# Output projections of a two-layer block: pairs of row tiles in seven quadrant products, with the gate row in the weights

## The reference, cut to what matters

```python
mix = jnp.concatenate([att, mlstm_out(h_sum, mo, mlstm_norm_w)], -1)
x = x + g1 * (mix @ w_out)                        # 2048 x 1024 by 1024 x 1024, g1 one row of 1024
hx2 = modulate(rmsnorm(x, norm2_w), sh2, sc2)
aff = jax.nn.softmax((h @ w_router).astype(f32), -1)   # in the expert layer, h = hx2
```

## Time and profile before

| | us |
|---|---|
| median of 3 runs | 4071.45 |
| lowest and highest run | 4067.83, 4078.97 |
| span of the profiled execution | 4066.4 |
| PE busy | 3776.7 (93%) |
| DVE busy | 1951.9 (48%) |
| ACT busy | 1561.1 (38%) |
| POOL busy | 547.7 (13%) |

### The profile page before, as it was taken

How to read it: one execution, slowest core, us unless ns; L and a number is a source line. 1 busy time by engine, 2 the same in 40 slices (tenths; PEclk the granted TensorE clock), 3 DMA queues, 4 the chain that set the end, 5 groups by cost and what they waited for, 6 DMA issues and landing times. The chain is left out here.

```text
span 4066.4 us, 63104 instructions
## 1 busy us (share of the span) xinstructions
PE 3776.7 (93%) x21839; PEld 2444.1 (60%) x21840; DVE 1951.9 (48%) x4191; ACT 1561.1 (38%) x3432; POOL 547.7 (13%) x746
## 2 busy tenths in 40 slices
PE   6999999799898978999999799997999999599998
PEld 4667766555584434777777677774666555344444
DVE  1334334556585553111111278776333444578886
ACT  1122211355564431111111266764333222267775
POOL 0000000100170010111111001101000000322222
PEclk8999999899999998999999899998999999699999
DMA  6222122222525477656656212115231133498974
GB/s 240 76 78 82 70 76 79 87 72 85 142 95 199 158 265 292 201 168 211 200 168 217 70 47 66 56 52 148 67 107 39 35 131 117 181 318 277 331 240 101
DMA packets 227153, 573.85 MB, mean 141 GB/s; under 512 B 28154, under 2 KB 100986, under 8 KB 211118
## 3 DMA queue, kind: packets, MB, share of 16 engines
q1 hardware_dynamic: 177742, 395.92, 27.7%
q0 software_dynamic: 49248, 175.79, 14.6%
HBM read 433.59 MB, written 137.93 MB: 141 GB/s over the span
## 5 line engine op out<-in xcount | busy, mean ns | idle before, releaser
L880 PE MATMUL inp_psU<-inp_w,inp_hT 128*128 128x512 f32 (+3 forms) x1376 | 420.8, 464 | 0.0
L880 PEld LDWEIGHTS inp_psU<-inp_w,inp_hT 128*128 128x128 f32 x1376 | 256.0, 190 | 152.7 <-issue 122.4
L4286 DVE COPY moe_bu<-moe_wu 128x1024 f32 x480 | 299.2, 697 | 39.2 <-DMA moe_wd<-in_w_down 22.5
L4173 PE MATMUL moe_psU<-moe_bu,shared_weights 128*32 128x256 f32 x3840 | 294.8, 382 | 0.9 <-issue 0.9
L4173 PE MATMUL moe_psU<-moe_wu,shared_weights 128*32 x1280 | 293.2, 382 | 1.8 <-DVE moe_bu L4286 1.7
L876 PE MATMUL inp_psU<-inp_hT,inp_w 128*128 128x256 f32 x1088 | 245.7, 386 | 10.2 <-DVE inp_tm L682 4.5
L2807 ACT ACTIVATE moe_sg<-moe_psG 128x256 f32<-128x256 f32 x64 | 24.6, 384 | 567.0 <-PE moe_psG L2766 567.0
L2824 DVE TENSOR_TENSOR moe_hT<-moe_sg,moe_psG 128x256 f32<-128x256 f32 x64 | 26.9, 421 | 437.7 <-ACT moe_sg L2807 437.7
L876 PEld LDWEIGHTS inp_psU<-inp_hT,inp_w 128*128 128x128 f32 x1088 | 209.0, 194 | 42.7 <-ACT inp_fm L773 3.9
L3502 PE MATMUL inp_psU<-shared_weights,inp_w 128*128 128x256 f32 x1024 | 231.9, 382 | 2.7 <-DMA inp_wg<-in_lru_wx 2.7
L2766 PE MATMUL moe_psG<-moe_xT,moe_u_w 128*128 128x256 f32 x1024 | 231.5, 379 | 0.0
(11 more groups left out here) (702 smaller groups left out, 7149.7 us busy)
## 6 DMA issues: line engine op xcount, KB each, us to landing
moe_wu<-in_w_up SPq DMA_DIRECT2D x32, 2048.0 KB
moe_d_w<-in_w_down SPq DMA_DIRECT2D x16, 2048.0 KB, 10.4
moe_wd<-in_w_down SPq DMA_DIRECT2D x32, 1024.0 KB
moe_u_w<-in_w_up SPq DMA_DIRECT2D x15, 2048.0 KB, 13.5
mod_w<-in_w_ada SPq DMA_DIRECT2D x24, 1024.0 KB, 13.2
inp_mod_w<-in_w_mod SPq DMA_DIRECT2D x16, 1024.0 KB, 4.9
xn<-out_xn POOLq DMA_DIRECT2D x32, 512.0 KB, 3.8
shared_weights<-in_w_gate SPq DMA_DIRECT2D x8, 2048.0 KB, 8.6
```

The lines of the kernel that those rows point to most:

```text
L880: mm = pe.matmul(psU[:, u % NB, 0:n], hT[:, par, k, j * P:(j + 1) * P], w[:, k, lo:lo + n], start=(k == 0), stop=(k == KD - 1))
L4173: mm = pe.matmul(psU[c, f, 0:2 * P], xT[:, p, k, c], w, start=(k == 0), stop=(k == KD - 1), tile_position=(0, g * LOT))
L4286: ins = dve.tensor_copy(bu[:, g - 1, f, c, :].rearrange("p k n -> p (k n)").unsqueeze(1), wu[:, bass.ds(slots[g - 1], 1), f, c, :].rearran ...
```

## The change

Tiles 0 and 1 are computed as before. From tile 2 on the tiles go in pairs (a, b), and the pair's product of 2 x 2 quadrants (two tiles by the two halves of `mixT`; the two halves of the weights' rows by two halves of columns) is made in seven products of quadrants in place of eight (Winograd's form of Strassen's scheme). Write Ad, An for tile a's direct and normed half, Bd, Bn for tile b's, and D0, D1, N0, N1 for the weights' quadrants. The row sums are left0 = Bd + Bn, left1 = left0 - Ad, left2 = An - left1, left3 = Ad - Bd (in place of Bd). The column sums, made once, are t1 = D1 - D0, t2 = N1 - t1, t4 = N0 - t2 and N1 - D1 (in place of D1). TensorE's products and VectorE's joins:

| product | of | joined into |
|---|---|---|
| P1 | Ad, D0 | part 0 (a copy) |
| P2 | An, N0 | x of a, columns 0 |
| P6 | left1, t2 | part 1 = P1 + P6 |
| P7 | left3, N1 - D1 | part 2 = part 1 + P7 |
| P5 | left0, t1 | part 3 = part 1 + P5, and x of b, columns 1 = part 2 + P5 |
| P3 | left2, N1 | x of a, columns 1 = part 3 + P3 |
| P4 | Bn, t4 | x of b, columns 0 = part 2 + P4 |

(In the scheme P4 carries a minus, which t4's sign takes in.) GpSimd makes the four row sums of each pair (`make_left`) and adds the residual x (`add_x`), which VectorE did. The gate row is no longer multiplied on each tile: at the stage's start VectorE multiplies it into the direct weights and GpSimd into the normed ones. `norm` is split into `square_mix` and `scale_mix`, `rest` into the joins and `finish`. All loops over tiles are written out. The modulation ring has 10 blocks in place of 12 and lends three of them for t1, t2 and t4 in out1, so that seven are loaded at its end and three after the last product. In layer 1 the gate row is loaded in the stage before, into the second row of the `x` buffer, so tile 1's x is loaded after the weights are multiplied.

```diff
-    RING = 12
+    RING, LENT = 10, 3
...
-        self.mix, self.mixT = tile("mix", [P, 2, 512]), tile("mixT", [P, 2, KD, P])
+        self.mix, self.mixT = tile("mix", [P, 2, 512]), tile("mixT", [P, 4, KD, P])
...
@@ VectorE @@
+            def room(t):
+
+                if t >= 2:
+                    dve.wait_ge(x_stored[t % 2], 32 * (t // 2))
+
+            def finish(t):
+                j = t % 2
+                if t < 2:
+                    dve.wait_ge(taken, 2 * t + 2)
+                else:
+                    dve.wait_ge(x_added, t - 1)
                 dve.tensor_tensor_reduce(out=sq[:, :], in0=xo[:, j, :], in1=xo[:, j, :], scale=1.0 / D,
...
+            dve.wait_ge(gr_landed, 16)
+            dve.wait_ge(direct_weights_landed, 32)
+            for h in range(2):
+                dve.tensor_tensor(w_direct[:, :, cols[h]], w_direct[:, :, cols[h]], gr[:, cols[h]].unsqueeze(1).to_broadcast([P, KH, BANK]),
+                                  ALU.mult).then_inc(direct_scaled, 1)
...
+            for q in range(1, PAIRS):
...
+                dve.wait_ge(made, made_by(q, P1))
+                if q > 1:
+                    dve.wait_ge(summed, 4 * q - 4)
+                dve.tensor_copy(part[:, 0, :], bank(q, P1)).then_inc(parted, 1)
+                room(a)
+                join(q, P2, xo[:, 0, cols[0]], part[:, 0, :], summed, n + 1)
+                if more:
+                    square_mix(c)
...
+                join(q, P6, part[:, 1, :], part[:, 0, :], parted, n + 1)
+                if more:
+                    scale_mix(c)
+                join(q, P7, part[:, 2, :], part[:, 1, :], parted, n + 2)
+                if more:
+                    square_mix(d)
...
+                join(q, P5, part[:, 3, :], part[:, 1, :], parted, n + 2)
+                room(b)
+                join(q, P5, xo[:, 1, cols[1]], part[:, 2, :], summed, n + 3)
+                if more:
+                    scale_mix(d)
+                join(q, P3, xo[:, 0, cols[1]], part[:, 3, :], summed, n + 4)
+                finish(a)
+                join(q, P4, xo[:, 1, cols[0]], part[:, 2, :], summed, n + 4)
+                finish(b)
@@ ScalarE @@
+            for q in range(1, PAIRS):
...
+                keep_turned(a - 2)
+                if more:
+                    gate(c)
+                    gate(d)
+                    root_mix(c)
...
+                keep_across(a - 2)
+                keep_turned(b - 2)
+                keep_logits(a - 2)
+                if more:
+                    root_mix(d)
+                    keep_mix(c)
...
+                keep_across(b - 2)
+                if more:
+                    keep_mix(d)
+                root_x(a)
+                keep_logits(b - 2)
+                root_x(b)
@@ TensorE @@
+            for q in range(1, PAIRS):
...
+                multiply(q, P1, direct_of(a), w_direct[:, :, cols[0]])
+                turn_xn(a - 2)
...
+                multiply(q, P2, normed_of(a), w_normed[:, :, cols[0]])
...
+                multiply(q, P6, left[:, 1, :, :], t2)
+                route_across(a - 2)
...
+                multiply(q, P7, direct_of(b), w_direct[:, :, cols[1]])
+                turn_xn(b - 2)
+                route(a - 2)
+                multiply(q, P5, left[:, 0, :, :], t1)
+                if more:
+                    turn(c)
+                multiply(q, P3, left[:, 2, :, :], w_normed[:, :, cols[1]])
+                route_across(b - 2)
+                if more:
+                    turn(d)
+                multiply(q, P4, normed_of(b), t4)
+                route(b - 2)
@@ GpSimd @@
+            def add_x(t):
+                q, j = t // 2, t % 2
+                pool.wait_ge(summed, 4 * q if j else 4 * q - 1)
+                pool.wait_ge(x_landed[j], nth(t))
+                pool.tensor_tensor(xo[:, j, :], xo[:, j, :], x[:, j, :], ALU.add).then_inc(x_added, 1)
...
+                pool.tensor_tensor(left[:, 0, :, :], direct_of(b), normed_of(b), ALU.add).then_inc(left_made, 1)
...
+            store(0)
+            for q in range(1, PAIRS):
+                store(2 * q - 1)
+                add_x(2 * q)
+                if q + 1 < PAIRS:
+                    make_left(q + 1)
+                add_x(2 * q + 1)
+                if q == PAIRS - 1:
+                    pool.drain()
+                store(2 * q)
+            store(NT - 1)
```

More of the change, by code:

```diff
@@ L1998, in out_projection @@
         fold = s.sb("fold", [P, n_logits])
+        left = s.sb("left", [P, 3, KH, P])
+        right = ring.lent() if ring else s.sb("right", [P, 3, KH * BANK])
+        t1, t2, t4 = (right[:, n, :].rearrange("p (k n) -> p k n", k=KH) for n in range(3))
         early_choice = RowChoice(nc, s, "early", 0, EARLY_ROWS, logits_out, picks) if picks else None
@@ L2020, in out_projection @@
[L2020 to L2035, removed]
+        direct, normed = rows.direct, 4 - rows.direct
@@ L2092, in norm, with scale_mix @@
                                   ).then_inc(msq, 1)
+            def scale_mix(t):
+                j = t % 2
+                ch = Chain(dve, dch, t, NF, NF - 3 if layer == 1 else NF - 2)
+                hv = mix[:, j, :]
+                hg = hv.rearrange("p (g d) -> p g d", g=NG)
                 dve.wait_ge(rooted, t + 1)
@@ new lines, in _ @@
+            square_mix(2)
+            scale_mix(2)
+            dve.wait_ge(normed_scaled, 2)
+            dve.wait_ge(right_dve, 1)
+            dve.tensor_tensor(t2, w_normed[:, :, cols[1]], t1, ALU.subtract).then_inc(right_dve, 1)
+            square_mix(3)
+            scale_mix(3)
+            for t in range(2):
+                first_rest(t)
+            for q in range(1, PAIRS):
+                a, b, c, d = (2 * q + n for n in range(4))
+                more = q + 1 < PAIRS
+                n = 4 * (q - 1)
+                dve.wait_ge(made, made_by(q, P1))
[6 more added lines that the diff above has]
+                    square_mix(c)
+                elif picks:
@@ L2203, in product @@
[L2203 to L2208 removed]
+                    pe.wait_ge(direct_scaled, h + 1)
+                    for k in range(KH):
+                        pe.matmul(psO[:, t, h, :], direct_of(t)[:, k, :], w_direct[:, k, cols[h]], start=(k == 0), stop=False)
@@ L2215, in product, with multiply @@
                 mm.then_inc(made, 1)
-            def turn(t, j):
+            def multiply(q, i, lhs, rhs):
+                n = 4 * (q - 1)
+                if q == 1 and i <= P7:
+                    pe.wait_ge(taken, i + 1)
+                elif i == P1:
+                    pe.wait_ge(parted, n - 1)
+                elif i in (P2, P6, P7):
+                    pe.wait_ge(summed, n - 3 + i)
+                elif i == P3:
+                    pe.wait_ge(summed, n + 1)
+                else:
+                    pe.wait_ge(parted, n + 1 if i == P5 else n + 2)
+                for k in range(KH):
+                    mm = pe.matmul(bank(q, i), lhs[:, k, :], rhs[:, k, :], start=(k == 0), stop=(k == KH - 1))
+                mm.then_inc(made, 1)
```

392 lines of the change are left out of this document (236 added, 156 removed).

## The result

The changed kernel takes 4087.74 us (median; 4086.49 to 4090.64), the kernel before 4075.21 beside it: ratio 1.0039, 95% interval 1.0027 to 1.0050: slower, where 7 us less had been forecast. (The two medians alone would give 1.0031; the four runs of the kernel before reach from 4067.83 to 4079.35.) The forecast was 4064 us, range 4041 to 4084.

The account below looks back on a forecast made before the run. TensorE bounds both output projections. Layer 1: 24.0 - 13.8 - 5.9 - 4.2 = 0.1 us gained; layer 2: 24.0 - 7.2 - 5.3 - 4.4 = 7.1; span 4066.4 to 4059.2, plus 5.0 gives 4064.2 us, range 4041 to 4084.

Parts of the forecast that it names:

- what layer 1's pairs give back: Six passages between out1's pairs, each 30.8 us instead of TensorE's 28.5: 13.8 us of the gain lost.
- The work removed: Output projections: seven pairs a stage each drop one 3.43 us product; 24.0 us a stage, 48.0 in all.
- Rival 3: Written-out instructions or more waits cost TensorE the 3.43 us back, about 4073 us; chance 0.10.
- The second ring: VectorE's queue, from `room` waiting for the `xn` store to the next P3 join: 30.8 us in layer 1, 29.8 in layer 2.
- rival 2: `xn` store lands later than 4.3 us and VectorE waits at `room(a)`; at 7 us, 4092 us; chance 0.15.
- The first ring: GpSimd's adds, tile b's root, then ScalarE's `keep_turned` of tile a delay TensorE: pairs of 30.2 and 30.6 us.
- The collision: In a pair, VectorE's row sum and `xn` block GpSimd's `make_left`, pushing it 1.8 to 2.0 us later.
- The start: Weight multiplications and sums delay each output stage's first products: 4.2 us in layer 1 (2 to 9), 4.4 in layer 2.
- The tails: After each stage's last product, tile b finishes behind tile a: 5.9 us more in layer 1, 5.3 in layer 2.
- At nothing: Later-loaded modulation blocks in the choosing stage, and `choose_experts` under the tail, were costed at 0.
- The 5.0 us from the span to the median: Amount added to the forecast profiled span, 4059.2 us, to get the forecast median, 4064.2.

Follow-up runs that it names:

- The third buffer: Against the changed kernel, `xo` gets three buffers instead of two and the `xn` store wait moves to just before `xn` is written; ratio to the kernel before 0.9975.

## Why the prediction was wrong

Two terms of the sum failed, by about as much: what layer 1's pairs give back (13.8 us, measured 24.4) and layer 1's start (4.2, measured 13.9).

**The work removed: right.** With the stalls gone five pairs take 143.04 and 147.53 us, 28.61 and 29.51 a pair against 28.5 and 29.4 worked out from the earlier trace rows. Rival 3, that written-out code costs TensorE time, is out by the same rows. (The eight records of 3.43 us are one quadrant, a quarter of a tile's products and not half as I wrote; the sum counts eight and seven of them rightly.)

**The second ring: the step that failed in the pairs.** I had the right wait: `room` in front of P2's join, "each us that the store lands later" paid again in every pair. But I priced the landing at 4.3 us from three early transfers and gave the later landing, rival 2, 0.15. It was 7.8. The stores came 11.9 us after P3 (1352.28, P3's end at 1340.4) rather than 13.2; the landing ate more than that. No median of before would have helped, since its steady pairs have 3.8 and no such burst. The change's own order shows it: each `load_x` is released by GpSimd's `x_added`, which is also just ahead of the store in its queue, and the direct loads stand right behind it. I had even written "the store is now in a burst with loads" and then let a median from another time decide. At 7 us rival 2's sum gave 4092, 4 us above the result; but it ascribed all to the pairs, and the runs show about 17 us lost in out1's five steady pairs and 3 in out2's, the rest in first pairs, starts and tails. That near hit is luck.

**How the wait reaches TensorE: half right.** I followed VectorE's own queue to the next P3. The runs show the shorter way: root, `keep_across`, folding, in ScalarE's order. Moving `square_mix` alone brought out2 to 29.5 us. VectorE's ring was also too long: the room opened at S+20.1 instead of S+18.1, which would make its 30.8 us 32.8, and the pairs without a slow product (last section) took 31.3.

**The first ring: wrong in size.** I took 30.2 and 30.6 us. The third buffer leaves GpSimd's work whole and gives 28.97 and 29.51, so in layer 1 it is some 1.2 us shorter and in layer 2 it doesn't bind at all. GpSimd's groups of the changed kernel (busy us, mean ns, idle before):

```profile
L2457 POOL TENSOR_TENSOR out_xo<-out_xo,shared_rows 128x1024 f32<-128x1024 f32 x13 | 30.5, 2348 | 117.2 <-DVE out_xo L2188 117.2
L2476 POOL TENSOR_TENSOR out_left<-out_left,out_mixT 128x512 f32<-128x512 f32 x6 | 12.8, 2131 | 0.5
L2480 POOL TENSOR_TENSOR out_left<-out_mixT,out_left 128x512 f32<-128x512 f32 x6 | 9.7, 1621 | 0.5
L2474 POOL TENSOR_TENSOR out_left<-out_mixT 128x512 f32<-128x512 f32 x6 | 7.7, 1279 | 0.0
L2481 POOL TENSOR_TENSOR out_mixT<-out_mixT 128x512 f32<-128x512 f32 x6 | 7.6, 1266 | 0.0
```

The price of the residual (2.34 us estimated, 2.35 measured) and of a free sum (1.27) was right. The collision was foreseen: VectorE's row sum takes 2.32 us beside `make_left` (1343.67) instead of 1.23. But it costs less: the four sums with their collisions are 6.3 us, where I had 5.4 and a further 1.8 to 2.0.

**The start: as large a miss.** 4.2 and 4.4 predicted, 13.9 and 7.5 measured, above the range of 2 to 9 in layer 1. I had priced GpSimd's 4.4 us instructions as a delay of 4.5 to one `turn`; there were three such meetings (5.05, 3.62 and 4.88 us for instructions of 0.7), and behind the third an order on ScalarE that I didn't follow: `root_x(0)` ahead of `keep_mix(2)`. The first pair, 34.5 us in layer 1, wasn't in the sum either: GpSimd's first store stood behind `make_left` and a 4.51 us difference, and VectorE waited 11.05 us for it.

**The tails: right in kind, 3 us short in layer 1.** 8.9 and 4.4 us more against 5.9 and 5.3; 8.9 is above the bound of 8. In layer 1 the last joins stood behind the same store until 1498.15, while the modulation blocks filled the transfers, and TensorE's clock in the tail was 0.57 (share 0.88 and clock in the table of stretches). How the 3 us divide among these was not tried.

**At nothing: right for this kernel.** The choosing stage takes 68.1 us after and 68.7 before, with 10 blocks in the ring instead of 12, three of them loaded late. The blocks do cost something once the tail is short: 8 to 13 us at the barrier behind out1 in the kernels with the mended tail, against 4.2 here. Whether `choose_experts` costs something was not tried by itself.

Of the sum, a gain of 7.2 us was forecast, and by the profiled spans a loss of 19 came; 9.7 of the difference are layer 1's start, 10.6 its pairs, the rest small terms of both signs. The 5.0 us from the span to the median were in part spread: each run of the kernel before takes 1.9 to 2.0 us more than its own span, each of the change 1.6 to 1.7. That is 3 us of the forecast and doesn't carry the miss.

## What to carry to other kernels

When a change makes a buffer's store later, look at which loads the same event releases, price the landing with those transfers beside it and not at a median of another time, and put a wait for it behind everything on its engine that another engine needs. A repeated stage hides a wrong order of two instructions only while nobody is late; each moved step is worth following to the first thing that stands behind it on every engine. Here 48 us of removed work became a gain of 34 once the buffer and the orders were mended, and without that a loss of 12.5 by the medians, some 16 by the ratio.

## What the runs showed of the hardware

A 512 KB store landed in 3.8 us with the loads held apart and in 7.8 with 1.5 MB more issued within the same 1.5 us (medians of ten). A VectorE instruction of 0.69 us took 5.05 beside GpSimd's instructions of 2048 columns, two in 9.43 us. Where two queues of long instructions met, with the weight differences on VectorE beside `make_left`, both grew: VectorE's 2048 columns took 3.35 to 3.39 us instead of 2.28, three of GpSimd's sums of 512 columns 3.20 to 3.32 instead of 1.27. It looks as if they took turns; the traces don't show how.

TensorE lost more than its gaps. After an idle of 2.03 us the next product took 5.2 us from start to start instead of 3.5, at a granted clock of 0.67, between the full level of 2.4 GHz and the lower of 1.2. After one of 1.68 us it did so again (5.2 us, 0.67), but after one of 1.87 us (1363.79, above) it did not: 3.5 us at 1.00. So the length of the gap alone doesn't decide it, and what does is open.

```profile
1330.98 0.40 PE L2402 MATMUL out_psL<-out_fold,out_lgT 128*128 128x16 f32 x2 [2.03 <-ACT out_lgT L2282]
1331.22 5.38 PE L2365 MATMUL out_psO<-mod_w,out_left 128*128 128x512 f32 x8
1336.44 0.60 PE L2373 MATMUL out_psM<-ident,out_mix 128*128 128x128 f32 x4
...
1426.51 0.40 PE L2402 MATMUL out_psL<-out_fold,out_lgT 128*128 128x16 f32 x2 [1.68 <-ACT out_lgT L2282]
1426.75 5.38 PE L2365 MATMUL out_psO<-mod_w,out_left 128*128 128x512 f32 x8
```

One such product is the difference between pairs of 31.3 and 33 us. The two slow products of the five pairs are some 3.5 of the 5.3 us by which TensorE is busier in the changed kernel (148.30) than without the stalls (143.04).
